# One mixer and mixture-of-experts layer: expert weights in runs of 16 KB per partition from the second pair on

## What is computed

```python
def expert_block(args):
    tok, e = args
    xb = x_pad[tok]                       # up to 64 tokens in this kernel
    gu = xb @ w_gu[e] + b_gu[e]           # (1024) x (1024, 2048)
    gate, up = gu[:, :D_FF], gu[:, D_FF:]
    gate = jnp.minimum(gate, SWIGLU_LIMIT)
    up = jnp.clip(up, -SWIGLU_LIMIT, SWIGLU_LIMIT)
    h = (up + 1.0) * gate * jax.nn.sigmoid(SWIGLU_ALPHA * gate)
    return h @ w_down[e] + b_down[e]      # (1024) x (1024, 1024)
```

## Time and profile before

| | us |
|---|---|
| median of three runs | 1174.92 |
| lowest and highest of them | 1173.86, 1175.33 |
| the profiled execution | 1173.83 |
| its span | 1171.8 |
| TensorE busy (PE) | 1109.4 (95%) |
| weights loads of TensorE (PEld), beside PE | 521.9 |
| moved by DMA | 436.10 MB, mean 372 GB/s |

### The profile page before, as it was taken

How to read it: one execution, slowest core, us unless ns; L and a number is a source line. 1 busy time by engine, 2 the same in 40 slices (tenths; PEclk the granted TensorE clock), 3 DMA queues, 4 the chain that set the end, 5 groups by cost and what they waited for, 6 DMA issues and landing times.

```text
span 1171.8 us, 13786 instructions
## 1 busy us (share of the span) xinstructions
PE 1109.4 (95%) x5376; PEld 521.9 (45%) x5376; DVE 298.5 (25%) x529; ACT 151.8 (13%) x245; POOL 96.4 (8%) x53
## 2 busy tenths in 40 slices
PE   8989999899999999999999898989899999999996
PEld 5879955535343434343434242424242424243432
DVE  3771664421212121121202020211112121212113
ACT  3242101011101011111010111111101010110101
POOL 3684420000000000000000000000000000000002
PEclk9989999899999999999999999999999999999998
DMA  9953375797999999999999999999999999999994
GB/s 355 328 187 109 118 290 197 273 422 309 419 418 415 420 415 422 413 422 413 422 413 422 413 421 414 421 414 422 413 423 413 421 414 421 415 420 415 419 417 187
DMA packets 94504, 436.10 MB, mean 372 GB/s; under 512 B 8784, under 2 KB 18768, under 8 KB 61488
## 3 DMA queue, kind: packets, MB, share of 16 engines
q1 hardware_dynamic: 87952, 428.68, 90.9%
q10 hardware_dynamic: 6528, 7.09, 1.7%
HBM read 431.78 MB, written 3.97 MB: 372 GB/s over the span
## 4 chain that ended last, share of the span: by engine, by line
PE 52%; SPq 22%; DMA 16%; DVE 6%; issue 3%; ACT 1%; DVEq 0%
PE bank L779 19%; SPq L388 13%; PE bank L796 11%; DMA ring<-w_down 9%; SPq L392 8%; DMA old_rooms<-w_down 6%; PE bank L481 5%; PE bank L737 3%; PE bank L608 3%; PE bank L862 3%; DVE zu L1113 1%; PE bank L508 1%; DVE biasp L1115 1%; PE bank L766 1%; ACT oo L988 1%
## 5 line engine op out<-in xcount | busy, mean ns | idle before, releaser
L779 PE MATMUL bank<-ring,xg 128*64 128x512 f32 x1536 | 337.2, 593 | 0.0
L779 PEld LDWEIGHTS bank<-ring,xg 128*64 128x64 f32 x1536 | 107.1, 137 | 207.7 <-issue 202.5
L796 PE MATMUL bank<-ring,act_t 128*64 128x512 f32 x768 | 176.6, 597 | 16.2 <-DMA ring<-w_down 16.1
L1399 DVE TENSOR_SCALAR gate_c<-bank 128x512 f32<-128x512 f32 x32 | 22.1, 692 | 395.1 <-PE bank L779 395.1
L779 PE MATMUL bank<-old_rooms,xg 128*64 128x512 f32 x512 | 112.8, 592 | 0.0
L796 PEld LDWEIGHTS bank<-ring,act_t 128*64 128x64 f32 x768 | 50.8, 136 | 123.2 <-issue 72.9
L737 PEld LDWEIGHTS bank<-onehot,hid 128*128 128x128 f32 x720 | 81.5, 192 | 12.2 <-issue 12.2
L1291 DVE CAST sel<-sel_all 96x128 bf16 (+1 forms) x16 | 3.6, 223 | 325.0 <-PE bank L862 325.0
L1047 POOL TENSOR_TENSOR rstd<-veps,minus_half 128x1 f32<-128x1 f32 x6 | 3.3, 548 | 986.3 <-DVE veps L1223 986.3
L737 PE MATMUL bank<-onehot,hid 128*128 128x128 f32 x720 | 84.4, 277 | 0.0
L1021 POOL TENSOR_TENSOR w_parts<-ring,w_parts 128x1024 fp32r<-128x1024 f32 x26 | 75.4, 2908 | 55.5 <-ACT w_parts L893 55.5
(11 more groups left out here) (199 smaller groups left out, 734.6 us busy)
## 6 DMA issues: line engine op xcount, KB each, us to landing
ring<-w_gu SPq DMA_DIRECT2D x192, 1024.0 KB, 24.3
ring<-w_down SPq DMA_DIRECT2D x96, 1024.0 KB, 19.7
old_rooms<-w_gu SPq DMA_DIRECT2D x64, 1024.0 KB, 20.5
old_rooms<-w_down SPq DMA_DIRECT2D x29, 1024.0 KB, 24.8
ring<-w_in SPq DMA_DIRECT2D x13, 1024.0 KB, 14.5
ring<-w_out SPq DMA_DIRECT2D x4, 1024.0 KB, 6.7
st<-s_ret SPq DMA_DIRECT2D x4, 512.0 KB, 10.8
lnp<-ln ACTq DMA_DIRECT2D x4, 512.0 KB, 7.7
```

The lines of the kernel that those rows point to most:

```text
L779: mm = pe.matmul(bank[2 * a + n][64 * hf:64 * hf + 64, :], xg[:, c, 64 * a:64 * a + 64], w[:, col:col + 512], start=False, stop=(c == KC - 1))
L796: mm = pe.matmul(bank[4][64 * hf:64 * hf + 64, :], act_t[:, a, c % 4, 64 * (c // 4):64 * (c // 4) + 64], w[:, c % 2, hf * 512:(hf + 1) * 5 ...
L1399: dve.tensor_scalar(gate_c[:, :], bank[2 * a][:, :], LIMIT, None, ALU.min).then_inc(gate_ready, 1)
```

## The change

From the second pair on (`turn` is not None), the weights come in runs of 2 MB. A run of `w_gu` is 256 consecutive rows, of which partition p gets rows 2p and 2p + 1; a run of `w_down` is 512 consecutive rows, of which partition p gets rows 4p to 4p + 3. Both are one stretch of 16 KB per partition, in memory and in the buffer, and fill two neighbouring rooms. SP issues 12 transfers for a pair, each waiting until both of its rooms are free (the bound is that of the later room). TensorE waits once per run, on the semaphore of the run's first room; it still raises `piece_used` per MB. The first pair keeps its pieces of 1 MB, but its `w_down` pieces have rows 2p and 2p + 1 on partition p, one stretch of 8 KB.

As the rows on a partition are now neighbours, a chunk of the contraction holds every second row (`w_gu`, all pairs but the first) or every fourth (`w_down`; every second in the first pair). So `gather` loads `hid` with a column step of 2 as its stationary operand, and the transposes load `act_h` with a step of 4 (2 in the first pair). The first pair's gather (`gather_first`) is as it was. No matmul is added or taken away.

```diff
+GU_RUN, DN_RUN = 2, 4
+GU_UNITS, DN_UNITS = GU_RUN, DN_RUN // 2
...
+        runs = [(j, GU_UNITS) for j in range(0, 2 * GU_PIECES, GU_UNITS)] \
+            + [(j, DN_UNITS) for j in range(2 * GU_PIECES, PAIR_PIECES, DN_UNITS)]
...
-                return sp.dma_start(dst.rearrange("p (k n) -> p k n", n=D), w_down[bass.ds(e, 1), k:k + 256, :]
-                                    .rearrange("e (k p) n -> p (e k) n", p=128))
+                return sp.dma_start(dst.unsqueeze(1), w_down[bass.ds(e, 1), k:k + 256, :]
+                                    .rearrange("e (p k) n -> p e (k n)", p=128))
+
+            def expert_run(j, ea, eb, dst):
+
+                if j < 2 * GU_PIECES:
+                    e, k = (ea, eb)[j // GU_PIECES], (j % GU_PIECES) * 128
+                    return sp.dma_start(dst.unsqueeze(1), w_gu[bass.ds(e, 1), k:k + 128 * GU_RUN, :]
+                                        .rearrange("e (p k) n -> p e (k n)", p=128))
+                i = j - 2 * GU_PIECES
+                e, k = (ea, eb)[i // DN_PIECES], (i % DN_PIECES) * 256
+                return sp.dma_start(dst.unsqueeze(1), w_down[bass.ds(e, 1), k:k + 128 * DN_RUN, :]
+                                    .rearrange("e (p k) n -> p e (k n)", p=128))
 
             def pair_pieces(first, ea, eb, odd, second=False):
 
-                for j in range(PAIR_PIECES):
+                for j, units in runs:
                     g = pair_fill(j, odd)
 
                     if second and j < WIDE:
-                        sp.wait_ge(piece_used, MIX_PIECES + piece_of.get(g - WIDE, g - WIDE + len(SIDE)) + 1)
+                        sp.wait_ge(piece_used, MIX_PIECES + 1 + max(piece_of.get(m - WIDE, m - WIDE + len(SIDE))
+                                                                    for m in range(g, g + units)))
                     else:
-                        sp.wait_ge(piece_used, first + (j - WIDE + 1))
-                    expert_piece(j, ea, eb, room(g % WIDE)).then_inc(slot_full[g % WIDE], 16)
+                        sp.wait_ge(piece_used, first + (j + units - WIDE))
+                    expert_run(j, ea, eb, rooms(g % WIDE, units)).then_inc(slot_full[g % WIDE], 16)
...
                         mm = pe.matmul(bank[6 + c // 4][:, (c % 4) * 128:(c % 4 + 1) * 128],
-                                       hid[:, t, c * 128:(c + 1) * 128], onehot[:, t, :],
+                                       hid[:, t, :].rearrange("p (q m k) -> p q k m", m=128, k=GU_RUN)
+                                       [:, c // GU_RUN, c % GU_RUN, :], onehot[:, t, :],
                                        start=(t == 0), stop=(t == NT - 1))
...
+            def run_landed(j, units, turn, odd):
+
+                g = pair_fill(j, odd)
+                once, per_turn = run_landings(g)
+                pe.wait_ge(slot_full[g % WIDE], 16 * per_turn * turn + 16 * once)
+                return rooms(g % WIDE, units)
...
                     mm = pe.transpose(bank[5][:, j * 128:(j + 1) * 128],
-                                      act_h[:, a, j * 128:(j + 1) * 128], ident)
+                                      act_h[:, a, :].rearrange("p (q m k) -> p q k m", m=128, k=run)
+                                      [:, j // run, j % run, :], ident)
...
-                    w = landed(GU_PIECES * a + c, turn, odd)
+                    if turn is None:
+                        w = landed(GU_PIECES * a + c)
+                    elif c % GU_RUN == 0:
+                        w_run = run_landed(GU_PIECES * a + c, GU_UNITS, turn, odd).rearrange("p (k n) -> p k n", n=2 * FF)
+                    if turn is not None:
+                        w = w_run[:, c % GU_RUN, :]
...
-                    if c % 2 == 0:
-                        w = landed(2 * GU_PIECES + DN_PIECES * a + c // 2, turn, odd)\
-                            .rearrange("p (k n) -> p k n", n=D)
+                    run = 2 if turn is None else DN_RUN
+                    if c % run == 0:
+                        j = 2 * GU_PIECES + DN_PIECES * a + c // 2
+                        w = landed(j) if turn is None else run_landed(j, DN_UNITS, turn, odd)
+                        w = w.rearrange("p (k n) -> p k n", n=D)
```

More of the change, by code:

```diff
@@ L286, in room, with rooms @@
             return ring[:, n, :] if n < RING else old_rooms[:, n - RING, :]
+        def rooms(n, units):
+            r = ring[:, n:n + units, :] if n < RING else old_rooms[:, n - RING:n - RING + units, :]
+            return r.rearrange("p a b -> p (a b)")
         mixer_fills = [sum(mixer_room(i) == n for i in range(1, MIX_PIECES)) if n < RING else 0 for n in range(WIDE)]
@@ L300, in pair_fill, with run_landings @@
             return FIRST_FILLS + (0 if odd else PAIR_PIECES) + j
+        runs = [(j, GU_UNITS) for j in range(0, 2 * GU_PIECES, GU_UNITS)] \
+            + [(j, DN_UNITS) for j in range(2 * GU_PIECES, PAIR_PIECES, DN_UNITS)]
+        run_rooms = [pair_fill(j, odd) for odd in (True, False) for j, _ in runs]
+        def run_landings(g):
+            n = g % WIDE
+            return mixer_fills[n] + sum(m % WIDE == n for m in range(FIRST_FILLS)) \
+                + sum(m % WIDE == n and m <= g for m in run_rooms), sum(m % WIDE == n for m in run_rooms)
         def mixer_wait(eng, i):
@@ L745, in gates, with landed, transpose_act @@
                 mm.then_inc(gt_mm, 1)
[L747 to L759, removed]
-                return room(g % WIDE)
-            def transpose_act(a, p):
+            def landed(j):
+                g = first_fill(j)
+                if g is None:
+                    pe.wait_ge(side_full[j], 16)
+                    return side[j]
+                pe.wait_ge(slot_full[g % WIDE], 16 * (mixer_fills[g % WIDE] + g // WIDE + 1))
+                return room(g % WIDE)
+            def run_landed(j, units, turn, odd):
[3 more added lines that the diff above has]
+                return rooms(g % WIDE, units)
+            def transpose_act(a, p, run):
                 pe.wait_ge(act_ready, 2 * p + a + 1)
@@ L797, in down @@
                                        act_t[:, a, c % 4, 64 * (c // 4):64 * (c // 4) + 64],
-                                       w[:, c % 2, hf * 512:(hf + 1) * 512], start=False, stop=(c == KC - 1))
+                                       w[:, c % run, hf * 512:(hf + 1) * 512], start=False, stop=(c == KC - 1))
                     if c % 2 == 1:
@@ L827, in pair @@
                 gate_up_bias(1)
-                gate_up(1, turn, odd, {4: lambda: transpose_act(0, p)} | ({2: count_before, 6: by_expert} if first else {}))
+                gate_up(1, turn, odd, {4: lambda: transpose_act(0, p, 2 if first else DN_RUN)} | ({2: count_before, 6: by_expert} if first else {}))
                 pe.wait_ge(act_t_ready, 2 * p + 1)
@@ L833, in pair @@
                     sums_so_far(2, 3)
-                down(0, turn, odd, {4: lambda: transpose_act(1, p)})
+                down(0, turn, odd, {4: lambda: transpose_act(1, p, 2 if first else DN_RUN)})
                 if last:
```

## The result

The changed kernel takes 1157.49 us (median of four runs, 1156.23 to 1159.16), the kernel before beside it 1174.39. The ratio is 0.986, with a 95% interval of 0.984 to 0.988. The forecast was 1158, range 1147 to 1171. The profiled execution took 1157.46 us, its span is 1155.4.

A forecast was written before the change was run, and what follows sets the result against it. Transfers set the pace of the second half, while the first only eats a lead. From 1173.83 us, -20.5 + 1.7 + 1.7 + 0.4 = -16.7 gave 1157.1, as a median 1158; range 1147 to 1171.

The forecast's parts named there:

- The pace of a run: Weight transfers from pair 2's down pieces on: 16 KB stretches move at 428.5 GB/s, a pair 58.73 us, -20.5 us.
- Coarse rooms: Waiting for two free rooms or 2 MB costs +1.7 us at the restart and +1.7 behind pair 15's last landing.
- Strided loads: Stationary loads with a column step: zero more for the gather, 0.4 us for the last pair's transposes, the others hidden.
- No second gap: Transfers at the end of pair 2, near 343 us: 1.7 MB still queue, so no new idle gap opens.
- First starvation: TensorE's first wait for a transfer comes near pair 10 and no longer in pair 7.
- No gain beyond 8 KB: Rival on weight transfers: 16 KB stretches win nothing over 8 KB, -4.6 us in all, 1170; chance 0.13.
- long runs slower: Rival on weight transfers: partitions reading 16 KB apart meet in memory; at 410 GB/s +18 us, 1193; chance 0.07.
- more than the line: Rival on weight transfers: gain beyond the fixed price per packet, at most -30.6 us, 1144 to 1152; chance 0.10.
- Strided gather slow: Rival on the gather: loads at 8 B step take twice the time, 5.5 us more per gather, +52, 1227; chance 0.11.

## Why the prediction was right, step by step

**The pace of a run.** Forecast 428.5 GB/s and 58.73 us a pair from three row lengths; measured 428 and 58.73. From SP's first issue behind the gap to pair 15's last landing it was 807.96 us, and is 787.23 (287.35 to 1074.58): -20.7 against -20.5. The rates at 8 KB (two runs) and the period at 32 KB lie on the same line, and so do the durations of single packets, so the extrapolation was one of a law and not of a point.

**Coarse rooms.** +1.7 at the restart: the issue moved from 1.76 to 3.48 us behind pair 2, 1.72. +1.7 behind the last landing: from landing to pair 16 it was 13.57 us and is 15.58, 2.0, of which 0.3 is the slower gather. Measured alone, with the old rows, the two came to 3.5.

**Strided loads.** I had zero for the gather; it took 0.3 us. It counts twice on the path, before pair 2 and behind the last landing. Pair 2 starts 0.44 later: the gather's 0.3, and nearly 0.2 from the first pair's two sets of transposes, which the sum did not have. For the last pair's transposes I had 0.4; from pair 16 to the end of the span it was 65.08 us and is 65.24, 0.16. These were the terms of the sum that were off, by +0.7 and -0.2. The zero came from the row of the contiguous gather, with the same columns and bytes. By that reasoning a step of 16 B would have been free too, and it cost 5.6 us more for each gather; only the page set the two steps apart. As far as it rests on the rows, that the zero was nearly right is luck, and so is the 0.4, a third of a bound with no strided load behind it.

**Sum.** -20.7 + 1.7 + 2.0 + 0.4 + 0.2 = -16.4, which is the difference of the spans (1171.8 to 1155.4); forecast -16.7.

**No second gap.** Windows from 335 to 350 us show 436, 424 and 426 GB/s: right. **First starvation** was forecast near pair 10, without a working, and came in pair 11. TensorE's spare time was taken as 2.1 us a pair; with the slower loads it is 58.73 - 57.09 = 1.64, and the lead lasts longer. With contiguous loads TensorE first waited in pair 9 (721.47 us).

**Rivals.** "No gain beyond 8 KB" and "long runs slower" fell with the 428 GB/s, and "more than the line" did too, as it is the line's own value. "Strided gather slow" did not happen at 8 B and happened at 16 B. The change stands one step from it.

## What to carry to other kernels

Where the rate of the transfers sets the end, fit the rate against packets per MB over the row lengths that the trace already has; two or three lengths give the price of a packet and the worth of the next doubling, and each doubling is worth half the one before. Set against it what grows with the transfer: the wait for several rooms at each restart, and the work behind the last landing. When a longer stretch on a partition forces strided stationary loads, look at the step in bytes first, since the next doubling of the row can cost far more than it brings, and measure it on that very load: the transposes' loads here did not tell the price of the gather's.

## What the runs showed of the hardware

- Each packet costs a fixed 9 to 10 ns on top of its bytes, by the rates from stretches of 2 KB (387 GB/s) over 4 (409), 8 (422) and 16 (428) to 32 KB (slices of 432). The single packets' own durations, 164, 314, 615 and 1217 ns from 4 to 32 KB, leave 12 to 13 ns. Half the transfers with the same stretches changed no rate.
- The gather's stationary loads of 128 fp32 columns, which follow each other, take 113 ns contiguous, 119 at a step of 8 B and 235 at a step of 16 B. Four transposes of the same width take 0.59 us contiguous and 0.68 at either step. The cliff is one of the gather's loads; why the transposes do not have it stays open.
- Behind the idle gap, transfers of 1 MB with stretches of 8 KB moved 373 to 389 GB/s in the 2 us windows from 288 to 294 (the run with the new rows in 1 MB), and 410 or more only from 294 on. With 2 MB at a time the changed kernel had 418 and 438 from 290 to 294.
